# Latent attention with its norm, modulation and input products as one unrolled program, in three-pass products and a pipeline two units deep

## What is computed

```python
def mla_mixer(h, cos, sin, w_in, q_norm, w_qb, kv_norm, w_kvb, w_o):
    z = h @ w_in
    cq = rms_norm(z[..., :Q_LORA], q_norm)
    ckv = rms_norm(z[..., Q_LORA:Q_LORA + KV_LORA], kv_norm)
    k_pe = apply_rope(z[..., Q_LORA + KV_LORA:], cos, sin)
    q = (cq @ w_qb).reshape(B, L, MLA_HEADS, QK_NOPE + QK_ROPE)
    kv = (ckv @ w_kvb).reshape(B, L, MLA_HEADS, QK_NOPE + V_DIM)
    ...
        s = (jnp.einsum('bqhd,bkhd->bhqk', qn, k_nope)
             + jnp.einsum('bqhr,bkr->bhqk', qp, k_pe)).astype(jnp.float32) * scale
        s = jnp.where(causal, s, jnp.float32(-1e30))
        p = jax.nn.softmax(s, axis=-1).astype(v.dtype)
        return jnp.einsum('bqhk,bkhd->bqhd', p, v)
```

## Time and profile before

| | |
|---|---|
| median of 3 runs | 4199.58 us (4198.38 to 4201.0) |
| profiled execution, its own time | 4198.77 us |
| its span in the trace | 4197.2 us |
| busy: PE / DVE / ACT / POOL | 3745.4 / 2309.8 / 1663.2 / 1153.5 us |
| last product of `peer` ends to first product of z | 2763.1 to 2799.35 us |
| z and latents, to the first projection of a head | 2799.35 to 2847.78 us |
| heads, to the last output copied | 2847.78 to 3010.78 us |
| first product of `ffn` | 3015.23 us |

### The profile page before, as it was taken

One profiled execution on the slowest core, in us unless ns is written; L12 is line 12 of the kernel. 1 busy time (PEld: TensorE's weight loads), 2 busy tenths in 40 slices (PEclk: granted clock), 3 DMA queues, 4 the chain that ended last, 5 costly groups with the idle time before them and its releaser, 6 DMA issues. The chain is left out here.

```text
span 4197.2 us, 46857 instructions
## 1 busy us (share of the span) xinstructions
PE 3745.4 (89%) x17722; PEld 3058.6 (73%) x17722; DVE 2309.8 (55%) x3536; ACT 1663.2 (40%) x2283; POOL 1153.5 (27%) x671
## 2 busy tenths in 40 slices
PE   2999989889799999999999999977789984678998
PEld 1888767767588888888788888844568873566886
DVE  6555444345366575576277777733453446755343
ACT  6555444444322244454344444423342231333222
POOL 0222122144144433333444444410020024603002
PEclk9999899999899999999999999988999996889999
DMA  4111021045133335444788888820122321122321
GB/s 152 56 51 55 11 68 46 11 165 205 56 129 130 127 122 198 188 155 142 282 266 268 266 265 265 265 79 27 40 74 96 96 75 36 38 81 71 100 96 65
DMA packets 226046, 516.20 MB, mean 123 GB/s; under 512 B 23312, under 2 KB 98320, under 8 KB 223664
## 3 DMA queue, kind: packets, MB, share of 16 engines
q1 hardware_dynamic: 202448, 407.83, 29.7%
q0 software_dynamic: 18864, 68.69, 5.0%
q10 hardware_dynamic: 4528, 36.89, 2.2%
HBM read 439.15 MB, written 69.21 MB: 121 GB/s over the span
## 5 line engine op out<-in xcount | busy, mean ns | idle before, releaser
L1125 PE MATMUL peer_banks<-peer_h_parts,peer_w_parts 128*128 128x512 f32 x3456 | 800.6, 392 | 18.0 <-POOL peer_w_parts L1451 18.0
L1125 PEld LDWEIGHTS peer_banks<-peer_h_parts,peer_w_parts 128*128 128x128 f32 x3456 | 646.5, 188 | 151.5 <-POOL peer_w_parts L1451 18.8
L1125 PE MATMUL peer_banks<-peer_act_parts,peer_w_parts 128*128 128x512 f32 x3072 | 699.3, 390 | 9.4 <-DVE peer_act_parts L1745 9.4
L1125 PEld LDWEIGHTS peer_banks<-peer_act_parts,peer_w_parts 128*128 128x128 f32 x3072 | 578.4, 188 | 130.2 <-issue 9.8
L1451 POOL TENSOR_TENSOR peer_w_parts<-peer_raw,peer_w_parts 128x1024 fp32r<-128x1024 f32 x144 | 345.0, 2396 | 574.1 <-ACT peer_w_parts L1579 574.1
L1125 PE MATMUL ffn_ps<-ffn_h_parts,ffn_w_parts 128*128 128x512 f32 x1920 | 445.7, 395 | 34.6 <-DVE ffn_h_parts L2248 19.2
L1125 PEld LDWEIGHTS ffn_ps<-ffn_h_parts,ffn_w_parts 128*128 128x128 f32 x1920 | 366.3, 191 | 114.2 <-issue 21.4
L1125 PE MATMUL ffn_ps<-ffn_hidden,ffn_w_parts 128*128 128x512 f32 x1920 | 439.6, 391 | 9.7 <-DVE ffn_hidden L2248 9.7
L1579 ACT ACTIVATE peer_w_parts<-peer_raw 128x1024 fp32r<-128x1024 f32 x272 | 286.9, 1055 | 390.9 <-PE peer_banks L1125 390.9
L1125 PEld LDWEIGHTS ffn_ps<-ffn_hidden,ffn_w_parts 128*128 128x128 f32 x1920 | 361.4, 188 | 87.0 <-issue 11.9
L175 POOL TENSOR_TENSOR peer_slab<-peer_slab 128x1024 f32<-128x1024 f32 x96 | 236.7, 2466 | 336.6 <-ACT peer_slab L182 336.2
(11 more groups left out here) (515 smaller groups left out, 5416.5 us busy)
## 6 DMA issues: line engine op xcount, KB each, us to landing
peer_raw<-in_peer_u SPq DMA_DIRECT2D x128, 512.0 KB, 3.4
peer_raw<-in_peer_v SPq DMA_DIRECT2D x128, 512.0 KB, 4.7
slots<-in_mlp_w SPq DMA_DIRECT2D x128, 512.0 KB, 3.3
peer_slab<-in_w_mod POOLq DMA_DIRECT2D x96, 512.0 KB, 4.1
peer_acts<-h SPq DMA_DIRECT2D x128, 256.0 KB, 2.2
peer_gates<-peer_slab ACTq DMA_DIRECT2D x16, 2048.0 KB, 16.6
peer_slab<-peer_acts SPq DMA_DIRECT2D x128, 256.0 KB, 5.0
peer_slab<-peer_gates SPq DMA_DIRECT2D x128, 256.0 KB, 5.5
```

Source lines behind the costliest of these rows:

```text
L1125: last = nc.tensor.matmul(out, w(a, k), x(b, k), start=start and k == ks[0] and n == 0, stop=stop and k == ks[-1] and n == 2)
```

## The change

It does five things.

1. The blocks `normf`, `mla_ahead`, `modulate`, `mla_in` and `mla_heads` go. The sum of squares for the norm moves to the end of `peer`: ACT squares a tile as soon as DVE has added it, PE sums them behind its last product, ACT takes Ln and Exp.
2. `mla` is one block, written out without loops. Scaling by the root is DVE's `scale(k)`, and gain and modulation are one ACT instruction with two vector operands, done twice (`normalized(k)`: the high part and the full value). The norm's gain is not in `K.x` any more, and `ffn` layer 0 multiplies its residual by `alpha_g` instead of `ALPHA`.
3. z and the projections of the heads are in three passes. POOL makes the low parts of z's weights, DVE those of the heads' weights (`wt_low`), after ACT's `wt_high`. The first two tiles of z go together over k, as the parts of `h` come.
4. Weights come earlier: four tiles of `mla_win` are loaded at the end of `peer` into the ring that `peer` and the later stages now share, and the first two heads' weights are loaded at the start of `mla`.
5. The 32 units of 128 queries run in a pipeline that is two deep over all heads: PE makes the scores of unit n+2 before it transposes unit n, with three probability buffers for two, two output banks for one, and the next head's projections spread over units 0, 1 and 2 of the present one. Projections write to three banks in turn.

```diff
-    def __init__(self, nc, stack, d):
-        self.d = d
-        self.raw = stack.enter_context(nc.sbuf_tensor("peer_raw", [P, self.R, KT * P], F32))
+    def __init__(self, nc, raw, d):
+        self.d, self.raw = d, raw
...
+            for s in range(R):
+                sp.wait_ge(v_lo, V_TILES - R + s + 1)
+                sp.dma_start(ring.raw[:, s, :], d["mla_win"][s]).then_inc(K.win_in[s], 16)
...
+            for k in range(KT):
+                pe.wait_ge(sq_done, k + 1)
+                last = nc.tensor.matmul(o_ps(0), K.ones[:], K.h[:, k, :], start=k == 0, stop=k == KT - 1)
+            last.then_inc(sum_done, 1)
...
+            for k in range(KT):
+                act.wait_ge(x_done, k + 1)
+                A(K.h[:, k, :], K.x[:, k, :], ACT.Square).then_inc(sq_done, 1)
+            act.wait_ge(sum_done, 1)
+            A(K.h[:, 0, :], o_ps(0), ACT.Ln, scale=1.0 / D, bias=EPS).then_inc(root, 1)
+            act.wait_ge(root, 1)
+            A(K.h[:, 0, :], K.h[:, 0, :], ACT.Exp, scale=-0.5).then_inc(root, 1)
+            act.wait_ge(root, 2)
...
-                st.do(V.scalar_tensor_tensor(out=K.x[:, k, :], in0=o_ps(k), scalar=K.mod[:, 40 + k:41 + k],
-                                             in1=K.x[:, k, :], op0=ALU.mult, op1=ALU.add))
+                V.scalar_tensor_tensor(out=K.x[:, k, :], in0=o_ps(k), scalar=K.mod[:, 40 + k:41 + k],
+                                       in1=K.x[:, k, :], op0=ALU.mult, op1=ALU.add).then_inc(x_done, 1)
...
+            if l == 0:
+                f = VEC["final_g"][0]
+                st.then(G.tensor_scalar(alpha_g[:], K.vec[:, f:f + KT], ALPHA, None, ALU.mult))
...
+            act.wait_ge(small, 1)
             for k in range(KT):
-                A(K.x[:, k, :], K.x[:, k, :], ACT.Copy, scale=ALPHA).then_inc(scaled, 1)
+                if l == 0:
+                    A(K.x[:, k, :], K.x[:, k, :], ACT.Copy, scale=alpha_g[:, k:k + 1]).then_inc(scaled, 1)
+                else:
+                    A(K.x[:, k, :], K.x[:, k, :], ACT.Copy, scale=ALPHA).then_inc(scaled, 1)
...
-    load_ahead(nc, K, "mla_ahead", lambda n: d["mla_wo"][n])
-    modulate(nc, K, 0)
-    with ExitStack() as c:
-        cq = c.enter_context(nc.sbuf_tensor("cq", [P, 2, T], F32))
-        ckv = c.enter_context(nc.sbuf_tensor("ckv", [P, T], F32))
-        kpe = c.enter_context(nc.sbuf_tensor("kpe", [P, T], F32))
-        csq = c.enter_context(nc.sbuf_tensor("csq", [P, T], F32))
-        mla_in(nc, K, d, cq, ckv, kpe, csq)
...
+            sp.dma_start(pos[:], d["positions"].partition_broadcast(P)).then_inc(pos_in, 16)
+            for h in range(2):
+                sp.dma_start(wts[:, h, :], d["mla_wh"][h]).then_inc(wt_in[h], 16)
+            sp.wait_ge(zw_lo, 1)
+            sp.dma_start(raw[:, 0, :], d["mla_win"][4]).then_inc(K.win_in[0], 16)
+            for s in range(1, 4):
+                sp.wait_ge(zw_lo, s + 1)
+                sp.dma_start(raw[:, s, :], d["mla_wo"][s]).then_inc(K.slots.ready[s], 16)
+            sp.wait_ge(zw_lo, ZT)
+            sp.dma_start(raw[:, 0, :], d["mla_wo"][0]).then_inc(K.slots.ready[0], 16)
+            for h in range(2, H):
+                sp.wait_ge(wt_lo, h - 1)
+                sp.dma_start(wts[:, h % 2, :], d["mla_wh"][h]).then_inc(wt_in[h % 2], 16)
...
+            G.tensor_tensor(gain[:], K.ops[:, 0, 0:KT], K.vec[:, f:f + KT], ALU.mult).then_inc(small, 1)
+            for t in range(ZT):
+                eng.wait_ge(zw_hi, t + 1)
+                G.tensor_tensor(zw[:, t, 1, :], raw[:, t % 4, :], zw[:, t, 0, :].bitcast(F32), ALU.subtract).then_inc(zw_lo, 1)
...
+            def z_tile(t, k, start, stop):
+                return parts_product(nc, z[t], lambda a, k: zw[:, t, a, k * P:(k + 1) * P], lambda a, k: hp[:, a, k, :], (k,), start, stop)
+
+            pe.wait_ge(zw_lo, 2)
+            for k in range(KT):
+                pe.wait_ge(h_lo, k + 1)
+                for t in range(2):
+                    last = z_tile(t, k, k == 0, k == KT - 1)
+                    if k == KT - 1:
+                        last.then_inc(z_done, 1)
+            for t in range(2, ZT):
...
+            def project(h, p):
+                pe.wait_ge(wt_lo, h + 1)
+                out = piece(h, p)
+                w = wp[:, h % 2]
+                if h == 0:
+                    pe.wait_ge(lat_lo, 1 if p in (KN_, VT_) else 3)
+                if h or p == VT_:
+
+                    if p == QN_:
+                        pe.wait_ge(qp_stored, h)
+                    else:
+                        pe.wait_ge(q_stored, {KN_: 3 * h - 1, QP_: 3 * h, VT_: 3 * h + 1}[p])
...
-                weigh(i, b, 1)
-                scores(i, b, 3)
-
-            with pe.Fori(0, H // 2 - 1) as i:
-                head(i, 0, (i, 1))
-                head(i, 1, (i + 1, 0))
-            head(H // 2 - 1, 0, (H // 2 - 1, 1))
-            head(H // 2 - 1, 1, None)
+            project(0, KN_)
+            project(0, QN_)
+            project(0, QP_)
+            scores(0)
+            project(0, VT_)
+            scores(1)
+            for n in range(U):
+                h, qt = divmod(n, TT)
+                if n + 2 < U:
+                    scores(n + 2)
+                if h + 1 < H:
+                    if qt == 0:
+                        project(h + 1, KN_)
+                        project(h + 1, QN_)
+                    elif qt == 1:
+                        project(h + 1, QP_)
+                    elif qt == 2:
+                        project(h + 1, VT_)
+                if n:
+                    output(n - 1)
+                weights(n)
+            output(U - 1)
...
+            def normalized(k):
+                act.wait_ge(e_done, k + 1)
+                shift = K.mod[:, 48 + k:49 + k]
+                A(hp[:, 0, k, :], K.x[:, k, :], ACT.Identity, scale=gain[:, k:k + 1], bias=shift).then_inc(h_hi, 1)
+                if k >= 2:
+                    act.wait_ge(h_lo, k - 1)
+                A(buf[:, k % 2, :], K.x[:, k, :], ACT.Identity, scale=gain[:, k:k + 1], bias=shift).then_inc(h_full, 1)
+
+            def wt_high(h):
+                act.wait_ge(wt_in[h % 2], 16 * (h // 2 + 1))
+                if h >= 2:
+                    act.wait_ge(p_done, 4 * (h - 1))
+                A(wp[:, h % 2, 0, :], wts[:, h % 2, :], ACT.Copy).then_inc(wt_hi, 1)
+
+            def store(h, p):
...
+            def store_t(n):
+                w = (n % TT + 1) * P
+                act.wait_ge(t_done, n + 1)
+                if n >= 2:
+                    act.wait_ge(o_done, n - 1)
+                A(probt[:, n % 2, 0:w], tr[:, 0:w], ACT.Copy).then_inc(t_stored, 1)
...
+            z_high(0)
+            z_high(1)
+            act.wait_ge(small, 1)
+            for k in range(KT):
+                normalized(k)
+                if k in (2, 4):
+                    z_high(k // 2 + 1)
...
+            for n in range(U):
+                h, qt = divmod(n, TT)
+                if n + 1 < U:
+                    exp(n + 1)
+                if h + 1 < H:
+                    if qt == 0:
+                        store(h + 1, KN_)
+                        store(h + 1, QN_)
+                    elif qt == 2:
+                        store(h + 1, VT_)
+                if qt == 0 and h:
+                    store_out(h - 1)
+                store_t(n)
+                if qt == 3 and h + 2 < H:
+                    wt_high(h + 2)
...
+            scale(0)
+            for k in range(KT):
+                if k + 1 < KT:
+                    scale(k + 1)
+                dve.wait_ge(h_hi, k + 1)
+                dve.wait_ge(h_full, k + 1)
+                V.tensor_tensor(hp[:, 1, k, :], buf[:, k % 2, :], hp[:, 0, k, :].bitcast(F32), ALU.subtract).then_inc(h_lo, 1)
...
+            normalize(0)
+            for n in range(U):
+                h, qt = divmod(n, TT)
+                if n + 1 < U:
+                    normalize(n + 1)
+                if qt == 1 and h + 1 < H:
+                    store(h + 1)
+                if n + 2 < U:
+                    logits(n + 2)
+                if qt == 3 and h + 2 < H:
+                    wt_low(h + 2)
+    K.slots.ahead = True
...
-        f = VEC["final_g"][0]
-        norm_phase(nc, K, "normf", [(K.x, K.x, T, K.vec[:, f:f + KT], None)])
+        K.slots = WeightSlots(nc, ctx, "slots")
+        K.win_in = [nc.alloc_semaphore(f"mla_win_in{s}") for s in range(WeightSlots.R)]
+        ring = PeerRing(nc, K.slots.raw, d)
+        norm_phase(nc, K, "norm2", [(K.x, K.h, T, K.gs_ffn, K.mod[:, 24:32])], load=ring.load_first)
+        peer(nc, K, d, ring)
         recycle(nc)
 
 
-        K.slots = WeightSlots(nc, ctx, "slots")
         mla(nc, K, d)
         recycle(nc)
         ffn(nc, K, d, 0)

```

More of the change, by code:

```diff
@@ L2493, in _, with bank, piece @@
+        def bank(b):
+            return banks[:, b * T:(b + 1) * T]
+        z = [bank(b) for b in range(ZT)]
+        sums = [bank(5), bank(6)]
+        sc = [bank(3), bank(4)]
+        tr = bank(0)
+        op = [bank(1), bank(2)]
```

(24 more changed lines are left out.)

439 lines of the change are left out of this document (166 added, 273 removed).

## The result

The changed kernel takes 4123.35 us (median of 4 runs, 4122.61 to 4124.97), the kernel before, on the same chip, 4199.74 (4198.38 to 4201.0): a ratio of 0.9821, 95% interval 0.9809 to 0.9832, or 76.4 us less. The forecast was 4127.

A forecast was written before the change was run, and what follows sets the result against it. PE's work and waits from `peer` to `ffn` were taken to bound: 19.1 + 36.8 + 118.8 + 4.45 = 179.2 against 252.1 us, 72.9 less, giving 4127. Own range 4119 to 4133 (chance 0.52); 8-in-10 range 4117 to 4150.

The forecast's parts named there:

- Joint 1: From `peer`'s last product to the first z product: 19.1 us after the change for 36.2 before, gain 17.1.
- that these add: Before the first z product, DVE scalings 1.6, POOL subtractions 4.9 and DVE subtraction 0.7 run without overlap: 7.3 us.
- z: z and latents, from first z product to first projection: 36.8 us after the change for 48.4, gain 11.6.
- The 1.5 for the cold clock: Added to z's time because PE comes cold from an idle of about 12 us.
- Heads: First projection to last copy's end: 118.8 us for 163.0; a steady head 14.2, with waits of 1.35 and 0.5.
- the 1.3 "for the 1%": Added to the heads' 117.5 us because the end-to-end schedule gave 18.4 a head against 18.6 read.
- Joint 2: From the heads' last copy's end to `ffn`'s first product: 4.45 us, unchanged by the edit.
- narrow products at 0.22: Rival: the heads' 128-column products cost the float32 price, 10.6 us more, 4137; chance 0.25.
- at 0.081: Rival: the heads' 128-column products are cheaper than 0.11, 2.8 us less, 4124; chance 0.08.
- DVE and POOL overlap: Rival: at z's start ACT then paces the pair of tiles, 6.2 us less, 4121; chance 0.07.
- The pipeline overlaps nothing: Rival: a head keeps 18.4 us, each unit waiting for its own softmax; 34 more, 4161; chance 0.05.
- PE stays at 1.2 GHz: Rival: halved clock in the stage, now bound by PE; 105 us more, 4232; chance 0.03.

The follow-up runs named there:

- z_parts_in_peer: Changed kernel with high and low parts of z's first four weight tiles made at the end of `peer`, low parts by POOL; 4123.87 us.
- norm_apart: Changed kernel with the norm's squares, sums, Ln and Exp back in their own block behind `peer`; 4131.61 us.
- z_parts_dve_warm: Changed kernel with z's first four tiles' parts made in `peer`, low ones by DVE, plus unread products keeping PE busy before z; 4116.71 us.
- wt_early: Changed kernel with weight parts of the next head but one made in the turn of unit 1, not unit 3; 4116.27 us.
- depth_one: Changed kernel with the pipeline one unit deep instead of two (scores of unit n+1 before transposing unit n); 4141.12 us.

## Why the prediction was right

- **Joint 1**: 19.1 forecast, 17.6 measured (2762.4 to 2779.98). Sums and handover to Ln 7.07 for 6.9; Ln to Exp 2.54 for 2.6; block change 1.66 for 2.3. The 7.3 to the first z product (its terms add to 7.2) was 6.5, by another chain: ACT's first high part until POOL began, 1.13, a term that the sum left out, then POOL's two low parts, 5.28. DVE's scalings and its subtraction, 2.3 in the sum, lay beside them, so the choice "that these add" was wrong there, and two errors in part made up for each other. One bound was read wrongly: the 3.7 from `peer`'s last addition to `normf`'s first square was no block change but POOL's drain (z_parts_in_peer, norm_apart). The prediction did not know of it; that the sums and Exp cover it in the changed kernel, by 5.2 us, was luck.
- **z**: 36.8 forecast, 34.6 measured. The pair took 15.1 for 16.4. DVE was held beside POOL (2.83, 1.73 and 2.88 for 0.69), but at three of its instructions and not at each of the 13. The 1.5 for the cold clock did not show: 0.50 was granted from 2780 to 2784, when PE waited for parts of h anyway. It costs 1.8 only once the parts are early (z_parts_dve_warm).
- **Heads**: 118.8 forecast, 119.05 measured (to the last copy's end, 2933.59). Narrow products 0.114 for 0.11; a head 14.45 for 14.2; the wait for `wt_low` 1.12 after the last record's end for 1.35 between starts, which compares as 1.29; the other 0.39, or 0.55, for 0.5. That the first is late weight parts is shown by wt_early. PE's own work in a head came out at 12.6 by starts for 12.3, 2.5 us in eight heads; the 1.3 "for the 1%" and a start and drain of 6.5 for 7.4 took that up. That the total met within 0.3 is partly luck, and so is that this execution lost nothing in the tail, where most of the others lost 0.8 to 2.2.
- **Joint 2**: 4.6 for 4.45 (2933.59 to 2938.19).
- **Rivals**: narrow products at 0.22, the price of two float32 records, and at 0.081 are both excluded by the 0.114; the Trainium skill's 81 ns at 128 columns (TensorE: Matmul & The Clock Gate, "Back-to-back issue gap") is not reached by this type here. "DVE and POOL overlap" falls with the 2.83 and 2.88, though the start was shorter. "The pipeline overlaps nothing" falls with the 14.45; depth_one says what the overlap is worth. The clock was 1.00 in the windows from 2815 to 2911, so "PE stays at 1.2 GHz" falls too: the 0.50 at the start of z was over by the heads.

The sum came out at 76.3 less (252.1 to 175.8) for 72.9: 1.5 in the first joint, 2.2 in z. What the prediction didn't see is that the edits do not all pull the same way: the three passes in the heads cost 3.3 to 4.8 as placed.

## What to carry to other kernels

Lay each engine's instructions end to end in program order with durations from the trace: here that gave a head's length within 0.3 us in six orders of the work, and told which wait would remain. When operands are prepared (rounded, split) one turn ahead, ask which first use sets the deadline; making them two turns earlier, or using them later, gave 7 to 9 us, more than the faster product did (3.5). Before a block boundary look at what each engine still does after its last instruction, in the rows of the boundary's own line; other work can hide that, or new work can expose it. And compare stages piece by piece: a lower clock in the last 8 us of the heads cost up to 2 us, which was as large as half of the effects here.
